# Twelve projections of a two-block model moved from behind a scan into it, their results kept in idle buffers

## The reference, cut to what matters

```python
hx = modulate(rmsnorm(x, norm1_w), sh1, sc1)
p = hx @ w_in                       # columns: xbc, dt | z (1536) | u_pool (512)
xbc = silu(dwconv_centred(p[..., :CONV_CH], conv_w, conv_b))
y_x = ssd_bidir(xbc, dt_x, dt_bias, a_log, d_skip, init_states)   # both directions, chunks of 128 tokens;
                                                                  # the start states come from the context (256 tokens)
u_pool = p[..., XBCDT_COLS + SSD_W:].reshape(b * rows, GRID_W, POOL_W)
y_pool = pool_mixer(u_pool, pool_w, pool_scale)   # per group g: (windowed mean - self) @ pool_w[g]
# mixer_out:
y_ssd = rmsnorm(y_x * silu(z), ssd_norm_w)
x = x + g1 * (concatenate([y_ssd, y_pool], axis=-1) @ w_out)
x = x + g2 * moe_ffn(modulate(rmsnorm(x, norm2_w), sh2, sc2), ...)
```

## Time and profile before

| what | value |
|---|---|
| median of 3 runs | 4045.22 us (4039.15 to 4045.79) |
| time of the profiled execution | 4038.55 us |
| its span, first to last instruction | 4036.8 us |
| TensorE busy | 3572.9 us (89%) |
| VectorE busy | 2408.2 us (60%) |
| ScalarE busy | 1725.4 us (43%) |
| GpSimd busy | 503.4 us (12%) |
| TensorE's mean granted clock | 0.916 |
| second block's convolution | about 1871 to 2106 us of the span |
| scan | 2124.8 to 2400.4 us |
| gate, pooling, output projection | 2397.9 to 2644 us |
| experts | from about 2717 us |

### The profile page before, as it was taken

The page is one execution under the profiler, slowest core; times in us unless marked ns, Lnnn a source line. Parts: engine busy times, 40 slices in busy tenths (PEclk is TensorE's granted clock), DMA queues, the critical chain, the costliest instruction groups (busy, mean ns, idle before and its releaser), DMA issues.

```text
span 4036.8 us, 43749 instructions
## 1 busy us (share of the span) xinstructions
PE 3572.9 (89%) x13692; PEld 2488.9 (62%) x13692; DVE 2408.2 (60%) x2911; ACT 1725.4 (43%) x2321; POOL 503.4 (12%) x623
## 2 busy tenths in 40 slices
PE   7978899999987899997886689959999999999996
PEld 3437468874446478875544454437777777777774
DVE  5333365556243375553337762048888889898895
ACT  2134142322143142233220112027778777877773
POOL 0000000000000000000000000014343434343440
PEclk9975899999966899997997789969999999999998
DMA  4202223331211223330110002239999999999994
GB/s 173 69 26 69 62 74 95 96 96 63 63 53 47 63 84 94 94 99 26 42 45 3 1 0 78 78 115 336 331 349 334 356 332 353 339 345 343 341 354 174
DMA packets 167552, 615.18 MB, mean 152 GB/s; under 512 B 18480, under 2 KB 18608, under 8 KB 166992
## 3 DMA queue, kind: packets, MB, share of 16 engines
q1 hardware_dynamic: 156768, 573.84, 40.3%
q0 software_dynamic: 10672, 39.85, 3.6%
HBM read 586.35 MB, written 27.26 MB: 152 GB/s over the span
## 4 chain that ended last, share of the span: by engine, by line
PE 64%; DVE 14%; DMA 8%; ACT 7%; issue 6%; POOL 0%; DVEq 0%; SPq 0%; ACTq 0%; POOLq 0%
PE bank L560 52%; PE bank L1023 9%; DMA sb_ring<-in_w 6%; DVE w_part L2257 2%; ACT w_part L1486 2%; DVE sb_rstd L1580 2%; DVE sb_work L2284 1%; DVE sb_work L2288 1%; DVE sb_work L2279 1%; PE bank L1031 1%; DVE sb_work L2281 1%; PE bank L992 1%; ACT sb_work L1194 0%; DVE sb_work L2019 0%; ACT sb_work L1223 0%
## 5 line engine op out<-in xcount | busy, mean ns | idle before, releaser
L2257 DVE TENSOR_TENSOR w_part<-sb_ring,w_part 128x1024 fp32r<-128x1024 f32 x762 | 893.5, 1223 | 125.9 <-ACT w_part L1486 125.5
L1486 ACT ACTIVATE w_part<-sb_ring 128x1024 fp32r<-128x1024 f32 x762 | 772.2, 1053 | 141.9 <-PE bank L1023 79.4
L1023 PE MATMUL bank<-w_part,xg_hi 128*128 128x512 f32 x2048 | 566.1, 398 | 0.0
L560 PE MATMUL bank<-h_hi,split_part 128*128 128x512 f32 x1408 | 443.4, 400 | 8.3 <-ACT h_hi L1293 8.3
L1023 PEld LDWEIGHTS bank<-w_part,xg_hi 128*128 128x128 f32 x2048 | 384.7, 189 | 89.7
L560 PE MATMUL bank<-sb_work,sb_ring 128*128 128x512 f32 (+4 forms) x864 | 333.1, 541 | 22.2 <-DVE sb_modv L1570 10.5
L1023 PE MATMUL bank<-w_part,xg_lo 128*128 128x512 f32 x1024 | 322.1, 396 | 0.0
L560 PEld LDWEIGHTS bank<-h_hi,split_part 128*128 128x128 f32 x1408 | 267.4, 190 | 74.9 <-issue 8.4
L560 PE MATMUL bank<-sb_work 128*128 128x64 f32 (+6 forms) x992 | 257.3, 466 | 48.7 <-DVE sb_work L1789 22.8
L1023 PE MATMUL bank<-w_part,act_hi 128*128 128x512 f32 x1024 | 284.6, 399 | 0.1
L560 PEld LDWEIGHTS bank<-sb_work,sb_ring 128*128 128x128 f32 (+3 forms) x864 | 163.4, 190 | 187.3 <-issue 158.2
(11 more groups left out here) (323 smaller groups left out, 4996.4 us busy)
## 6 DMA issues: line engine op xcount, KB each, us to landing
sb_ring<-in_w SPq DMA_DIRECT2D x768, 512.0 KB, 7.1
sb_ring<-in_wstream SPq DMA_DIRECT2D x304, 512.0 KB, 3.5
y_rows<-sb_padc POOLq DMA_DIRECT2D x1, 4096.0 KB, 27.2
sb_xT<-in_x SPq DMA_DIRECT2D x1, 2048.0 KB, 11.4
x_rows<-sb_padc SPq DMA_DIRECT2D x1, 2048.0 KB, 22.5
x_rows<-sb_work SPq DMA_DIRECT2D x1, 2048.0 KB, 12.7
sb_work<-y_rows SPq DMA_DIRECT2D x4, 512.0 KB, 5.2
out_h<-sb_xT SPq DMA_DIRECT2D x1, 2048.0 KB, 6.3
```

What stands on the lines that cost most here:

```text
L560: ins = nc.tensor.matmul(out, l, r, start=start, stop=stop)
L1023: ins = nc.tensor.matmul(out[n][:], l[:, k, :], r[:, n * 512:(n + 1) * 512], start=False, stop=(k, p) == (KD - 1, 2))
L1486: nc.scalar.activation(w_hi[t % SPLITS], ring[:, t % RING, :], ACT.Copy).then_inc(s_hi, 1)
L2257: nc.vector.tensor_tensor(w_lo[t % SPLITS], ring[:, t % RING, :], w_hi[t % SPLITS].bitcast(F32), ALU.subtract).then_inc(s_lo, 1)
```

## The change

Eight of the twelve gate projections (`Z_BESIDE`) and all four pooling projections are issued by TensorE earlier. Each x step gets one gate projection between `cb` and `segments(0)`. Pooling projection 0 stands behind the convolution, 1 behind `total`, 2 in the third context step ahead of its state products, and 3 in the first x step ahead of its gate projection (`POOL_BEFORE`).

Their raw results need a place until the scan is over. ScalarE copies a pooling result into the convolution's pads (`pool_raw`, in `padc` and `pads`), and a gate result into `hT`. For that the residual is stored to DRAM by a DMA of 2 MB from GpSimd's queue, issued when the first block's last norm is out, and loaded back after the eighth product with a gate (semaphore `s_res`, 16 and 32). VectorE waits for the second one before its first update of `hT`.

Behind the scan ScalarE takes the silu of the eight stored gates in place and copies the pooling results into `pool_in`; the last four gate projections go as before. The squares of token block b stand behind the silu of the next block, VectorE makes the pooling windows between the gate products, and `pooled` has four slots instead of two.

```diff
--- before.py
+++ after.py
...
+        residual = nc.dram_tensor("residual", (P, KD * T), F32, kind="Internal").ap()
...
+        xw_at = place[0]
...
-        pooled = xs[:, 0:2 * T].rearrange("p (r t) -> p r t", t=T)
+        pooled = work[:, xw_at + 2 * T:xw_at + 6 * T].rearrange("p (r t) -> p r t", t=T)
+        pool_raw = [a[:].rearrange("p a t -> p (a t)")[:, i * T:(i + 1) * T] for a in (padc, pads) for i in range(2)]
...
+            pool.wait_ge(act_done, when("norm_out", ("ln2", DEPTH - 1), KD - 1))
+            pool.dma_start(residual.rearrange("p (k t) -> p k t", t=T), hT[:]).then_inc(s_res, 16)
+            pool.wait_ge(s_res, 16)
+            pool.wait_ge(dve_done, when("gated", Z_BESIDE - 1))
+            pool.dma_start(hT[:], residual.rearrange("p (k t) -> p k t", t=T)).then_inc(s_res, 16)
...
+            after_conv = state["stream"]
+            z_tiles = 4 * (SSD_W // 512)
+
+            def pool_projection(g):
+                w = loaded(after_conv + z_tiles + g).rearrange("p (k m) -> p k m", m=P)
+                chunks(("pool", g), lambda k: w[:, k, :], lambda k: xT[:, k, :], KD)
+                used()
+
+            def gate_projection(cg, b):
+
+                out = bank("z", cg, b)
+                for k in range(KD):
+                    if b == 0 and k % 2 == 0:
+                        state["z", k // 2] = loaded(after_conv + 4 * cg + k // 2).rearrange("p (k n) -> p k n", n=512)
+                    mm(out[:], xT[:, k, b * P:(b + 1) * P], state["z", k // 2][:, k % 2, :], k == 0, k == KD - 1,
+                       *(("z", cg, b) if k == KD - 1 else ()))
+                if b == TB - 1:
+                    used(4)
+
+            pool_projection(0)
             pe.wait_ge(dve_done, when("la"))
             out = bank("cs")
             for b in range(NB):
...
                     mm(out[:, a:a + SSD_HEADS], tri, la[:, b, d * SSD_HEADS:(d + 1) * SSD_HEADS], True, True,
                        *(("cs",) if (b, d) == (NB - 1, 1) else ()))
             mm(bank("total")[:, 0:NB * DT_W], ones, la.rearrange("p b n -> p (b n)"), True, True, "total")
...
+            pool_projection(1)
             pe.wait_ge(act_done, when("conv_out", "x", XC + 2 * GROUPS - 1))
             for s, (d, kind, b) in enumerate(SCAN):
+                if kind == "c" and s in POOL_BEFORE:
+                    pool_projection(POOL_BEFORE[s])
                 if kind == "x":
                     c_of = lambda g: c_t[:, g, b * P:(b + 1) * P]
                     out = bank("cb", s)
                     for g in range(GROUPS):
                         mm(out[:, g * P:(g + 1) * P], b_t[:, g, b * P:(b + 1) * P], c_of(g), True, True,
                            *(("cb", s) if g == GROUPS - 1 else ()))
+                    if s in POOL_BEFORE:
+                        pool_projection(POOL_BEFORE[s])
+                    gate_projection(*divmod(s - 2 * CB, TB))
...
-            for cg in range(SSD_W // 512):
-                ws = [tile().rearrange("p (k n) -> p k n", n=512) for _ in range(4)]
-                for b in range(TB):
-                    out = bank("z", cg, b)
-                    for k in range(KD):
-                        mm(out[:], xT[:, k, b * P:(b + 1) * P], ws[k // 2][:, k % 2, :], k == 0, k == KD - 1,
-                           *(("z", cg, b) if k == KD - 1 else ()))
-                used(4)
-            for g in range(4):
-                w = tile().rearrange("p (k m) -> p k m", m=P)
-                chunks(("pool", g), lambda k: w[:, k, :], lambda k: xT[:, k, :], KD)
-                used()
-            w = tile()
+            for i in range(Z_BESIDE, SSD_W // 512 * TB):
+                gate_projection(*divmod(i, TB))
+            w = loaded(after_conv + z_tiles + 4)
             for g in range(4):
                 pe.wait_ge(dve_done, when("pooled", g))
-                mm(bank("poolw", g)[:], w[:, g * P:(g + 1) * P], pooled[:, g % 2, :], True, True, "poolw", g)
+                mm(bank("poolw", g)[:], w[:, g * P:(g + 1) * P], pooled[:, g, :], True, True, "poolw", g)
             used()
+            state["stream"] = after_conv + z_tiles + 5
...
+            def pool_out(g):
+                act.wait_ge(pe_done, when("full", "pool", g))
+                act.wait_ge(dve_done, when("conv", "x", XC + 2 * GROUPS - 1))
+                act.wait_ge(act_done, did.n)
+                nc.scalar.activation(pool_raw[g], bank_of("pool", g)[:], ACT.Copy).then_inc(act_done,
+                    did.up(("free", "pool", g), ("pool_out", g)))
+
+            pool_out(0)
...
+            pool_out(1)
             for s, (d, kind, b) in enumerate(SCAN):
+                if s in POOL_BEFORE:
+                    pool_out(POOL_BEFORE[s])
                 if kind == "x":
+                    i = s - 2 * CB
+                    act.wait_ge(s_res, 16)
+                    act.wait_ge(pe_done, when("full", "z", *divmod(i, TB)))
+                    act.wait_ge(act_done, did.n)
+                    nc.scalar.activation(hT[:, i, :], bank_of("z", *divmod(i, TB))[:], ACT.Copy).then_inc(act_done,
+                        did.up(("free", "z") + divmod(i, TB)))
                     for g in range(GROUPS):
...
-            for cg in range(SSD_W // 512):
-                for b in range(TB):
...
-            for b in range(TB):
-                act.wait_ge(dve_done, when("gated", (SSD_W // 512 - 1) * TB + b))
+            for i in range(Z_BESIDE):
                 act.wait_ge(act_done, did.n)
...
+                nc.scalar.activation(hT[:, i, :], hT[:, i, :], ACT.Silu).then_inc(act_done, did.up(("z_silu", i)))
             act.wait_ge(dve_done, when("pool_pads"))
             for g in range(4):
                 if g >= 2:
                     act.wait_ge(dve_done, when("pooled", g - 2))
-                act.wait_ge(pe_done, when("full", "pool", g))
                 act.wait_ge(act_done, did.n)
-                nc.scalar.activation(pool_in[:, g % 2, :, POOL_PAD:POOL_PAD + GRID_W], bank_of("pool",
-                    g)[:].rearrange("p (r t) -> p r t", t=GRID_W), ACT.Copy).then_inc(act_done, did.up(("free",
-                    "pool", g), ("pool_kept", g)))
+                nc.scalar.activation(pool_in[:, g % 2, :, POOL_PAD:POOL_PAD + GRID_W], pool_raw[g].rearrange("p (r t) -> p r t", t=GRID_W), ACT.Copy).then_inc(act_done, did.up(("pool_kept", g)))
+
+            def row_squares(b):
+                act.wait_ge(dve_done, when("gated", Z_BESIDE + b))
+                act.wait_ge(act_done, did.n)
+                nc.scalar.activation(sq[:, 0:3, :].rearrange("p k t -> p (k t)"), ytok[:, b, :], ACT.Square,
+                    accum_out=sumsq[:, b:b + 1]).then_inc(act_done, did.up())
+
+            for i in range(Z_BESIDE, SSD_W // 512 * TB):
+                act.wait_ge(dve_done, when("gated", i - 2) if i >= Z_BESIDE + 2 else when("scan_done"))
+                act.wait_ge(pe_done, when("full", "z", *divmod(i, TB)))
+                act.wait_ge(act_done, did.n)
+                nc.scalar.activation(zs[:, i % 2, :], bank_of("z", *divmod(i, TB))[:], ACT.Silu).then_inc(act_done,
+                    did.up(("free", "z") + divmod(i, TB), ("z_silu", i)))
+                if i > Z_BESIDE:
+                    row_squares(i - 1 - Z_BESIDE)
+            row_squares(TB - 1)
+            act.wait_ge(act_done, did.n)
+            nc.scalar.activation(rs_tok[:], sumsq[:], ACT.Sqrt, bias=const("eps2"),
+                scale=1.0 / SSD_W).then_inc(act_done, did.up(("tok_dev",)))
...
             nc.vector.memset(pool_in, 0.0).then_inc(dve_done, did.up(("pool_pads",)))
-            for cg in range(SSD_W // 512):
-                for b in range(TB):
-                    i = cg * TB + b
-                    dve.wait_ge(act_done, when("z_silu", i))
-                    v = ytok[:, b, cg * 512:(cg + 1) * 512]
-                    dve.wait_ge(dve_done, did.n)
-                    nc.vector.tensor_tensor(v, v, zs[:, i % 2, :], ALU.mult).then_inc(dve_done, did.up(("gated", i)))
...
-            for g, window in enumerate(POOL_WINDOWS):
-
+            def gated(i):
+
+                cg, b = divmod(i, TB)
+                dve.wait_ge(act_done, when("z_silu", i))
+                v = ytok[:, b, cg * 512:(cg + 1) * 512]
+                dve.wait_ge(dve_done, did.n)
+                nc.vector.tensor_tensor(v, v, hT[:, i, :] if i < Z_BESIDE else zs[:, i % 2, :],
+                    ALU.mult).then_inc(dve_done, did.up(("gated", i)))
+
+            def pool_window(g):
+
+                window = POOL_WINDOWS[g]
                 dve.wait_ge(act_done, when("pool_kept", g))
-                if g >= 2:
-                    dve.wait_ge(pe_done, when("full", "poolw", g - 2))
...
+            for i in range(Z_BESIDE):
+                gated(i)
+            for g in range(3):
+                pool_window(g)
+            gated(Z_BESIDE), gated(Z_BESIDE + 1)
+            pool_window(3)
+            gated(Z_BESIDE + 2), gated(Z_BESIDE + 3)
```

(10 more changed lines are left out.)

22 lines of the change are left out of this document (2 added, 20 removed).

## The result

The changed kernel takes 3944.87 us (median of 4 runs, 3940.33 to 3951.65), the kernel before on the same chip 4042.18 (4 runs): ratio 0.9763, 95% interval 0.9745 to 0.9781. Forecast were 3949, between 3928 and 3974. The profiled execution after is the longest of its four, 3951.65 with a span of 3949.9, and all that follows is read from it. In five runs on another chip the median was 3951.49, ratio 0.9777 (0.9764 to 0.9791).

What follows compares the result with a forecast made beforehand. TensorE's projections bound the stretch behind the scan, VectorE the scan, where TensorE idles 6.99 us per step. Terms -83.9 + 3.8 - 1.4 - 11.2 = -92.7 us gave 3945.9 or 3952.5; 3949 was taken, range 3928 to 3974.

Steps and rivals of the forecast that it cites:

- S to the transposes: From S, the start of TensorE's work behind the scan, to the transposes: 121.5 us becomes 37.6, a gain of 83.9.
- end of the convolutions to the first seg matmul: Context steps and start of the first x step: projections that overrun their waits make it 3.8 us later.
- first x step from there: First x step, from its first seg matmul: seg matmuls at the full clock give back 1.4 us.
- seven x steps: Seven full scan steps: each gains 1.4 us at the first seg matmuls and 0.2 behind, 11.2 in all.
- transposes: Behind the scan: they start after an idle gap at the low clock as before (7.03 us), so no difference.
- I take 0.2 us per step as gain, between 0 and 1.7: Second half of each x step, from the third seg_in product to the next state scaling: a gain of 0.2 us.
- Rival (a): Clock stays up through the whole scan: 1.5 us more per step, up to 8 elsewhere, total 3930; chance 0.16.
- a step of 30 us or more: In the scan, a sign of being wrong: the seven steps were to take some 28.7 us each.
- products 0 and 1 give back 1.8 us each: Context steps: state products behind pooling projection 1 run at the full clock, near 2.7 us instead of 4.50.
- 1.3 late: First x step: pooling projection 3 and gate projection 0 take 13.8 us in TensorE's wait of 12.45 behind cb.
- rival (c): Behind the scan, the residual's reload comes too late for VectorE's hT update: 4042 and more; chance 0.02.
- S + 58: Behind the scan: when the reloaded residual is first needed, 58 us after TensorE's work starts; later output tile 0 meant wrong.

Runs made afterwards that it cites:

- e8: Changed kernel with pooling projections 1 and 2 moved and two useless matmuls ahead of each x step's third seg matmul: 3938.63 us (5 runs), ratio 0.9742.
- e7: Changed kernel with pooling projection 1 ahead of the sum of la and 2 behind gate projection 11: 3947.61 us (5 runs), ratio 0.9759.
- e2: Kernel before, no work moved, with eight useless matmuls between cb and the first seg matmul of each x step: 4029.02 us (5 runs), ratio 0.9961.
- e6: Changed kernel with two useless matmuls ahead of the third seg matmul of each x step: 3945.18 us (5 runs), ratio 0.9758.
- e9: Changed kernel with four useless matmuls ahead of each of state products 1 and 3 in the context steps: 3952.9 us (5 runs), ratio 0.9776.
- e3: Changed kernel with eight useless matmuls in front of each gate projection inside the scan: 4026.2 us in a single run.
- e4: Changed kernel with pooling projection 1 ahead of the sum of la instead of behind total: 3952.0 us in a single run.
- e1: Changed kernel with gate projections in the first four x steps only, the other eight behind the scan: 3993.4 us in a single run.

## Why the prediction was right, and where it was not

| term | forecast | traces |
|---|---|---|
| S to the transposes | -83.9 | -83.6 (121.53 to 37.94) |
| end of the convolutions to the first seg matmul | +3.8 | +6.8 |
| first x step from there | -1.4 | +0.1 |
| seven x steps | -11.2 | -13.95 |
| transposes | 0 | +1.1 |
| sum | -92.7 | -89.6 |

The starts before are those of the chain of waits; the timeline has the transposes 0.2 us sooner, which moves 0.2 us from one of these two terms to the other. With 1.1 us by which the convolutions ended sooner this is -90.7, and the output projection starts 90.70 us sooner (2526.24 to 2435.54). From there to the experts it stays so. The expert stage then took 1319.5 us before and 1323.2 after; the change doesn't touch it. In it some stretches are granted 0.98 and others 1.00, and a kernel's runs differ by up to 14 us (e8). This row is of before and this one of e8:
```profile
3117.32:3317.32 200.00, 188.91 (x857) 151.53 (x856) 178.76 (x182) 157.50 (x178) 79.99 (x95) 1.00 0.95 343
```
```profile
3011.29:3211.29 200.00, 188.00 (x840) 150.74 (x839) 175.07 (x179) 153.66 (x173) 78.20 (x95) 0.98 0.94 338
```
2% fewer matmuls fit into the second. That this is what spreads the runs is likely, but was not tried.

- **Behind the scan**: right, to 0.3 us, since the new bound was built as a chain of its own instead of subtracting 82.6 us of TensorE. The transposes start cold as before, but stay cold longer (8.09 us for 7.03 in the chains; the mean granted clock is 0.66 for 0.74); in e7, with the wait ahead of them filled, they run at 1.00. I had taken 0.
- **In a step**: the projection fits, at the full clock (0.1 us of slack), and brings 1.4 us. The second half was mis-sized: "I take 0.2 us per step as gain, between 0 and 1.7". It was 0.6 in the mean, but no step is at the mean: 27.2 or 31.0. e2 shows the whole 14 us as clock; e6 that the remaining 2.5 us of waiting makes the cold ones. Rival (a) was thus right for five steps of seven, and the forecast's own sign of being wrong, "a step of 30 us or more", came in the other two, by the clock and not by an overrun.
- **Context steps**: this is the step that failed. The forecast had the clock full from projection 1 on ("products 0 and 1 give back 1.8 us each", "products 2 and 3 give back 2.5"). Products 1 and 3 stand behind a wait, start cold and took 4.5 us as before. From the start of the sums to cb the context steps grew by 5.6 us instead of 3.8: products 0 and 1 give back 1.9 instead of 3.6, products 2 and 3 give back 1.5 instead of 2.5, and the two projections cost 0.9 less than reckoned. e9 confirms the cause (both products 2.74 us with the wait filled), and shows that mending it alone is worth nothing. The other 1.2 of the 3.0 us that this row is off lie in the first x step: the "1.3 late" behind cb, which the forecast names and then puts at nothing in "I count 3.8 for all of it".
- **First x step**: 1.4 gained in its first half, lost again in its second, which was at the full clock before and is partly at the low one after.
- **Residual**: right; 8.0 us to landing where 30 were allowed, so rival (c) had no ground. The first hT update comes at S + 59.8, later than the S + 58 that was named as a sign of being wrong, but it waits for TensorE (transposes and output tile 0), not for the reload.
- **Size of the total**: the profiled executions give 4038.55 - 3951.65 = 86.9, the medians 97.3 and 89.1. The terms above, the earlier convolutions and the longer expert stage make -89.6 - 1.1 + 3.7 = -87.0 of the first; what lies between it and the medians is from run to run. The sum came within 3.1 us because errors of both signs stood in it: the seven steps gained 2.75 more than forecast, the other four rows together 5.9 less. That part is luck.

The Trainium skill (TensorE: Matmul & The Clock Gate, section "What's actually happening") has the clock low unless activity lifts it; e2 agrees, with 14 us gained by eight matmuls per x step that compute nothing, while e3, which has still more of them, has the low clock in all second halves. What decides which second halves turn cold behind the same wait of 2.50 us stays open.

## What to carry to other kernels

A hole of one engine that another engine's chain makes is worth twice for TensorE: the work moved into it, and the clock behind it. Size what you move against the hole, since everything over it is paid in full (in e3 cold second halves came on top). When a stretch loses work, build its new end as a chain (here: last silu, squares, root, scaling) and count from its start, and where a wait of some 2.5 us is left ahead of a stretch, price it both warm and cold: here it was cold in two steps of seven, in state products 1 and 3, and in part of the first x step. A gain made by warming one place can be lost at the waits behind it: e9 filled two context waits, gained 2.2 us there and lost it in the first x step, while e6, with the waits of all x steps filled, kept its 7.5 us in the trace.

## What the runs showed of the hardware

- A wait of 2.50 us ahead of the same four matmuls left the granted clock at 1.00 in five steps and let it fall to 0.50 in two, in the same steps (second and fifth) in both traces of the kernel and in e2's. With another timing upstream it fell in others: the third and seventh in e9, the third and sixth in e7, the fourth alone in e4. With 0.73 us of waiting (e6) it fell in none of eight.
- More work does not always keep the clock: with 14 us of matmuls behind cb in each step (e3) every one of the seven second halves ran at the low level, with 7 us two of seven. The spacing of the waits changed too, and no run holds it fixed.
- With 7 us of matmuls in its hole and the wait of 2.50 us left, each of the seven steps took 27.2 us warm or 31.0 with a cold second half, and nothing between, in four kernels alike to 0.05 us (the changed kernel, e1's first three, e2, e9). With the hole open, before, they took 28.56 to 31.61.
- A store of 2 MB from SBUF to DRAM landed 7.7 us after issue from GpSimd's queue, the load back 8.0, while four other transfers of the same size from SyncE's took 11.5, 22.6, 12.6 and 6.3, so 2 MB have no single price here.
